# Leading tokens' and context's chains in another order, and three tiles' sums read later

## The reference

```python
y, k, v = token_mixer(h, ...)
x = x + gt1 * rmsnorm(y, g_post_mix)
h = rmsnorm(x, g_pre_ffn) * (1 + sc2) + sh2
aff = softmax(h @ w_router)                 # token x expert
g, idx = top_k(aff.T, cap)                  # cap 64 of 512 latents, 16 of 128 context tokens
hid = silu(xe @ w_gate) * (xe @ w_up)       # xe = h[idx]; width 2816
out = zeros.at[idx].add((hid @ w_down) * g)
x = x + gt2 * rmsnorm(out, g_post_ffn)
```

## Time and profile before

| | |
|---|---|
| time, median of 3 runs | 1947.46 us (1947.1 to 1952.33) |
| time of the profiled execution | 1953.02 us |
| its span, first to last instruction | 1951.2 us |
| PE busy | 1910.8 us, 98% of the span |
| DVE, ACT, POOL busy | 459.4, 301.4, 144.7 us |
| moved by DMA | 644.51 MB, mean 330 GB/s |

### The profile page before, as it was taken

How to read it: one execution, slowest core, us unless ns; L and a number is a source line. 1 busy time by engine, 2 the same in 40 slices (tenths; PEclk the granted TensorE clock), 3 DMA queues, 4 the chain that set the end, 5 groups by cost and what they waited for, 6 DMA issues and landing times.

```text
span 1951.2 us, 36708 instructions
## 1 busy us (share of the span) xinstructions
PE 1910.8 (98%) x16641; PEld 888.6 (46%) x16641; DVE 459.4 (24%) x825; ACT 301.4 (15%) x548; POOL 144.7 (7%) x216
## 2 busy tenths in 40 slices
PE   6999999999979999999999999999999999999997
PEld 3889787779853333323333333333333333333322
DVE  3432355557352101111010111101111110110114
ACT  4222245444220000000000000000000000000001
POOL 1000000000121101001010100101010010100004
PEclk9999999999979999999999999999999999999999
DMA  8851111112569999999999999999999999999997
GB/s 350 336 198 63 46 50 55 44 53 88 233 262 366 412 420 413 418 414 419 413 412 420 413 418 414 419 414 413 420 412 417 414 418 407 413 414 413 418 400 290
DMA packets 101412, 644.51 MB, mean 330 GB/s; under 512 B 11760, under 2 KB 14208, under 8 KB 43408
## 3 DMA queue, kind: packets, MB, share of 16 engines
q1 hardware_dynamic: 93792, 618.23, 77.5%
q0 software_dynamic: 6608, 20.85, 3.4%
q10 hardware_dynamic: 864, 3.15, 0.4%
HBM read 625.66 MB, written 16.52 MB: 329 GB/s over the span
## 4 chain that ended last, share of the span: by engine, by line
PE 96%; DVE 1%; DMA 1%; POOL 1%; issue 0%; ACT 0%; SPq 0%; POOLq 0%; DVEq 0%; ACTq 0%
PE ps L892 94%; PE ps L1073 1%; DMA out<-fin 1%; DMA x<-in_x_sample 0%; PE ps L995 0%; PE ps L1210 0%; PE ps L900 0%; PE ps L929 0%; DVE Gs L1921 0%; POOL rsx L733 0%; DVE topi L2095 0%; POOL rsx L732 0%; DVE topv L2094 0%; PE ps L1103 0%; DVE work L2097 0%
## 5 line engine op out<-in xcount | busy, mean ns | idle before, releaser
L892 PE MATMUL ps<-ring,xeT 128*32 128x512 f32 (+1 forms) x9216 | 914.4, 557 | 0.0
L892 PEld LDWEIGHTS ps<-ring,xeT 128*32 128x32 f32 x9216 | 296.9, 110 | 609.8 <-issue 608.5
L892 PE MATMUL ps<-ring,hidT 128*32 128x512 f32 x4224 | 459.6, 592 | 3.1 <-DMA ring<-in_w_dn 3.1
L892 PEld LDWEIGHTS ps<-ring,hidT 128*32 128x32 f32 x4224 | 136.1, 110 | 317.4 <-issue 310.8
L2233 DVE TENSOR_TENSOR hid<-sil,ps 128x768 f32<-128x768 f32 (+1 forms) x48 | 42.6, 887 | 915.1 <-ACT sil L1708 915.1
L1708 ACT ACTIVATE sil<-ps 128x768 f32<-128x768 f32 (+1 forms) x48 | 36.4, 758 | 959.9 <-PE ps L892 959.9
L892 PE MATMUL ps<-hT_hi,gq_hi 128*128 128x320 f32 x256 | 88.1, 344 | 0.0
L892 PE MATMUL ps<-in_hi,hT_hi 128*128 128x384 f32 x240 | 82.2, 343 | 0.0
L892 PE MATMUL ps<-in_lo,hT_hi 128*128 128x384 f32 x240 | 80.4, 335 | 0.0
L892 PE MATMUL ps<-in_hi,hT_lo 128*128 128x384 f32 x240 | 80.3, 335 | 0.0
L892 PE MATMUL ps<-hT_hi,gq_lo 128*128 128x320 f32 x256 | 79.1, 309 | 0.0
(11 more groups left out here) (262 smaller groups left out, 1432.0 us busy)
## 6 DMA issues: line engine op xcount, KB each, us to landing
ring<-in_w_gu SPq DMA_DIRECT2D x256, 1024.0 KB, 27.1
ring<-in_w_dn SPq DMA_DIRECT2D x176, 1024.0 KB, 24.1
ring<-in_w_gu_rest SPq DMA_DIRECT2D x128, 768.0 KB, 24.1
slab_y<-in_w_mod_blocks SPq DMA_DIRECT2D x8, 2048.0 KB, 8.9
in_slab<-in_w_in_blocks SPq DMA_DIRECT2D x6, 1536.0 KB, 8.7
gq<-in_w_gates SPq DMA_DIRECT2D x16, 512.0 KB, 3.4
slab<-in_w_mod_blocks SPq DMA_DIRECT2D x3, 2048.0 KB, 16.3
x<-in_x_sample SPq DMA_DIRECT2D x8, 512.0 KB, 6.4
```

The source lines that it names most:

```text
L892: return pe.matmul(out, lhsT, rhs, start=first, stop=last, **kw)
```

## The change

The diff has these parts.

- `aff_T(2)` and `aff_T(3)` are called after 4 of `out_proj(4)`'s 16 steps, not after 5.
- The first round of choice reads the affinities from PSUM and writes `work` by its replace; the copy goes. `row_list(0)` comes ahead of the fourth round's replace, and no longer waits for `y_done`, since its list `fG` lies elsewhere.
- Tile 4: ACT copies the projection unscaled (`y_copied`) ahead of squaring it, the square's dump goes to `xq[0]`; POOL issues `gather(0)` ahead of `rstd`; POOL only multiplies by the gain; DVE scales and adds the residual in one instruction, between rounds 5 and 6 (the rounds count from 0). ACT makes both halves of `h2T`.
- `first_tokens(0)` is done ahead of round 7, `first_tokens(2)` ahead of the tables' copies.
- `first_gate_up` has 16 units of group 0 first, then 8 + 4 of group 1, then group 2.
- At the end ACT loads the sums of tiles 2, 3 and 4 and the row of gains behind the first two tiles' squares, the last SILU, and the landing of load 556 of 0 to 559.

```diff
             for i, t in enumerate(LATE):
-                pool.wait_ge(y_sq, i + 1)
-                rstd(rsy[:, i:i + 1], ssy[:, i:i + 1], D, EPS).then_inc(y_rs, 1)
                 if t == NL:
...
                     gather(0, first_gathered)
+                pool.wait_ge(y_sq, i + 1)
+                rstd(rsy[:, i:i + 1], ssy[:, i:i + 1], D, EPS).then_inc(y_rs, 1)
+                if t == NL:
                     pool.wait_ge(gg_ev, 4)
-                    pool.wait_ge(y_scaled, 1)
+                    pool.wait_ge(y_copied, 1)
                     pool.tensor_tensor(row[0][:, :], row[0][:, :], ggrow[:, 1, :], ALU.mult).then_inc(y_used, 1)
-                    pool.wait_ge(ld_x[NL], 32)
-                    pool.wait_ge(y_used, NT)
-                    pool.tensor_tensor(x1[:, home(NL), :], x1[:, home(NL), :], row[0][:, :], ALU.add).then_inc(x1_ready, 1)
...
             def first_gate_up():
                 pe.wait_ge(x_add, 1)
-                first_part(0, range(1), (0,))
+                first_part(0, range(3), (0,))
                 second_rows()
-                first_part(0, range(1, 3), (0,))
                 router(NT - 1)
-                first_part(0, range(3, 7), (0,))
+                first_part(0, range(3, 6), (0,))
                 aff_T(NT - 1)
-                first_part(0, range(7, KD), (0,))
-                first_part(1, range(2), (0,))
+                first_part(0, range(6, KD), (0,))
+                first_part(1, range(5), (0,))
                 context_rows()
-                first_part(1, range(2, 4), (0,))
+                first_part(1, range(5, KD), (0,))
                 pe.wait_ge(x_add, 2)
                 first_part(0, range(4), (1,))
                 tables_T()
                 first_part(0, range(4, KD), (1,))
+                first_part(1, range(4), (1,))
                 pe.wait_ge(x_add, 3)
                 first_part(0, range(KD), (2,))
-                for k in range(KD):
-                    first_part(1, (k,), (1, 2) if k < 4 else (0, 1, 2))
+                first_part(1, range(4), (2,))
+                first_part(1, range(4, KD), (1, 2))
...
-            for t in LAST:
+            def sums_rows(t):
                 act.wait_ge(w_used, FREE + t // 2)
                 act.dma_start(fin[t][:, :], ysum_dram[t * P:(t + 1) * P, :]).then_inc(ld_x[t], 16)
+            for t in LAST[:2]:
+                sums_rows(t)
+            act.wait_ge(xs_ready, E_)
+            for i in range(2):
+                tokens_square(i)
+            silu(last, 2)
+            late = len(FLOW_W) - 4
+            act.wait_ge(w_ld[late % RS], 16 * (late // RS + 1))
+            for t in LAST[2:]:
+                sums_rows(t)
             act.wait_ge(gg_loaded, 16)
             act.wait_ge(w_used, FREE + 3)
             rows = gg_dram[KD:2 * KD, :].rearrange("(o k) p -> o (k p)", o=1)
             act.dma_start(gg_c[:, :], rows.to_broadcast([P, D])).then_inc(gg_loaded, 16)
-            act.wait_ge(xs_ready, E_)
-            for i in range(2):
-                tokens_square(i)
-            silu(last, 2)
             for i in range(2, NT):
                 tokens_square(i)
...
-            for r in range(4):
+            v8, i8, all_ = topv[:, 0:8], topi[:, 0:8], ps[0:E_, 7, :]
+            link(dve.max(v8, all_))
+            link(dve.max_index(i8, v8, all_))
+            link(dve.match_replace(work[:, :], v8, all_, -1.0))
+            dve.sem_inc(affT_used, 1)
+            for r in range(1, 4):
+                choose(work, LAT, 0, r, r < 3)
+            row_list(0)
+            v8 = topv[:, 24:32]
+            link(dve.match_replace(work[:, :], v8, work[:, :], -1.0))
+            first_index(0)
+            for r in range(4, 6):
                 choose(work, LAT, 0, r, True)
-            dve.wait_ge(y_done, NT)
-            row_list(0)
...
+            dve.wait_ge(ld_x[NL], 32)
+            dve.wait_ge(y_rs, NT)
+            dve.wait_ge(y_used, NT)
+            dve.scalar_tensor_tensor(x1[:, home(NL), :], row[0][:, :], rsy[:, 4:5], x1[:, home(NL), :],
+                                     ALU.mult, ALU.add).then_inc(x1_ready, 1)
+            choose(work, LAT, 0, 6, True)
             dve.wait_ge(first_gathered, 16)
             first_tokens(0)
+            choose(work, LAT, 0, 7, False)
             row_list(1)
-            h2_low(NT - 1)
```

More of the change, by code:

```diff
@@ L279, in program @@
         xs = at("xs", E0 + 47104, [P, 3, 256])
-        fG = at("fG", E0 + 11264, [E_, 3, 4, 32])
+        fG = [at("fG_lat", 117760, [E_, 2, 4, 32]), at("fG_ctx", E0 + 11264, [E_, 1, 4, 32])]
         yrA, yrB = at("yrA", E0 + 4096, [P, 512]), at("yrB", E0 + 6144, [P, 512])
@@ L302, in program @@
         topi = at("topi", 117440, [E_, CT], U32)
-        topf = at("topf", E0 + 49792, [E_, CT])
         S0 = [E0 + 53248]
@@ L326, in program @@
         work_c = small("work_c", [E_, CTX])
+        topf = small("topf", [E_, CT])
         idxT = small("idxT", [P, 3, E_], I32)
@@ L378, in program @@
             sem(n) for n in ("idxg_set", "idxs_set", "gathered", "scattered"))
-        first_gathered, first_turned, y_scaled = sem("first_gathered"), sem("first_turned"), sem("y_scaled")
+        first_gathered, first_turned, y_copied = sem("first_gathered"), sem("first_turned"), sem("y_copied")
         pool_turn = sem("pool_turn")
@@ L1255, in _ @@
             router(3)
-            out_proj(4, 3, 5)
+            out_proj(4, 3, 4)
             aff_T(2)
             aff_T(3)
-            out_proj(4, 5, 16)
+            out_proj(4, 4, 16)
             def rows_T(bank_, g):
-                return pe.transpose(ps[:, bank_, g * E_:(g + 1) * E_], fG[:, g, :, :].rearrange("e x j -> e (x j)"),
+                return pe.transpose(ps[:, bank_, g * E_:(g + 1) * E_], fG[g // 2][:, g % 2, :, :].rearrange("e x j -> e (x j)"),
                                     par[0:E_, 0:E_])
@@ L1647, in y_square @@
                 b = 2 * (i % 2)
-                act.activation(row[i % 2][:, :], ps[:, b:b + 2, :].rearrange("p b n -> p (b n)"), ACT.Square, scale=0.5,
+                if i == NT - 1:
+                    act.wait_ge(x2_stored[0], 32)
+                dump = xq[0] if i == NT - 1 else row[i % 2]
+                act.activation(dump[:, :], ps[:, b:b + 2, :].rearrange("p b n -> p (b n)"), ACT.Square, scale=0.5,
                                accum_out=ssy[:, i:i + 1]).then_inc(y_sq, 1)
@@ L1691, in _ @@
             l_exp(3)
+            act.wait_ge(y_done, NT)
+            act.activation(row[0][:, :], ps[:, 0:2, :].rearrange("p b n -> p (b n)"), ACT.Copy).then_inc(y_copied, 1)
             y_square(4)
-            act.wait_ge(y_rs, NT)
-            act.activation(row[0][:, :], ps[:, 0:2, :].rearrange("p b n -> p (b n)"), ACT.Copy,
-                           scale=rsy[:, 4:5]).then_inc(y_scaled, 1)
             x1_square(4)
             h2_high(4)
+            act.activation(h2T[0][:, 0:4, :], ps[:, 4, :].rearrange("p (k t) -> p k t", k=4), ACT.Copy).then_inc(h2_v, 1)
             quarters(4)
@@ L2117, in _ @@
             dve.wait_ge(affT_done, NL)
-            dve.tensor_copy(work[:, :], ps[0:E_, 7, :]).then_inc(affT_used, 1)
-            dve.wait_ge(affT_used, 1)
             def scaled(c, g0, g1):
@@ L2142, in row_list @@
                 for x in range(4):
-                    last = dve.tensor_scalar(fG[:, g, x, :], topi[:, 32 * g:32 * g + 32], 4.0, float(x), ALU.mult, ALU.add)
+                    last = dve.tensor_scalar(fG[0][:, g, x, :], topi[:, 32 * g:32 * g + 32], 4.0, float(x), ALU.mult, ALU.add)
                 link(last)
@@ L2149, in first_index @@
                 dve.tensor_copy(idx_g[g][:, :], ps[:, 7, g * E_:g * E_ + 1]).then_inc(idxg_set, 1)
-            for r in range(4):
-                choose(work, LAT, 0, r, True)
-            dve.wait_ge(y_done, NT)
-            row_list(0)
[L2155 to L2161, removed]
+            v8, i8, all_ = topv[:, 0:8], topi[:, 0:8], ps[0:E_, 7, :]
[10 more added lines that the diff above has]
+            for r in range(4, 6):
+                choose(work, LAT, 0, r, True)
+            dve.wait_ge(ld_x[NL], 32)
[4 more added lines that the diff above has]
+            choose(work, LAT, 0, 6, True)
             dve.wait_ge(first_gathered, 16)
             first_tokens(0)
+            choose(work, LAT, 0, 7, False)
             row_list(1)
-            h2_low(NT - 1)
             first_index(1)
@@ L2177, in _ @@
                 for n in range(2):
-                    last = dve.tensor_scalar(fG[:, 2, x, CC * n:CC * (n + 1)], topi[:, CL:CT], 4.0, float(4 * LAT + x),
+                    last = dve.tensor_scalar(fG[1][:, 0, x, CC * n:CC * (n + 1)], topi[:, CL:CT], 4.0, float(4 * LAT + x),
                                              ALU.mult, ALU.add)
@@ L2197, in _ @@
             dve.sem_inc(tab_ready, 1)
+            dve.wait_ge(gathered, 16)
+            first_tokens(2)
             dve.wait_ge(tabT_done, 4)
@@ L2207, in _ @@
             dve.wait_ge(tab_set, 1)
```

(2 more changed lines are left out.)

## The result

The changed kernel took 1964.59 us (median of 4 executions, 1961.66 to 1966.31), the kernel before, beside it, 1949.55 us (4, 1947.10 to 1952.33). The ratio is 1.0071, with an interval from 1.0051 to 1.0091. So the change costs about 14 us. The forecast said slower, by 9.2 us, and put the end of its range at 1962.0 us; the measured median is 2.6 us above that. A later comparison with more executions gave 1.0074 (1.0059 to 1.0090). The profiled execution took 1966.31 us with a span of 1964.5, against 1953.02 and 1951.2 before: 13.3 us more span.

What follows compares the result with a forecast made beforehand. The saturated weight stream was taken as the bound, PE living on a shrinking cushion. Late rows cost 9.2 us, containing the front's gain of 0.7 and the stream's lateness of 4.1: median 1947.5 to 1956.7 us, range 1946.5 to 1962.

Steps and rivals of the forecast that it cites:

- Cost of this part: 1946.5 + 13.9: At the end, late rows: tile 4 finished at 1946.5, then 13.9 us of work to 1960.4, 9.2 us more.
- SP issues a load when the slot 18 loads back is used up, so at PE's pace: Weight stream: loads issued at PE's pace but delivered ever later, 6.0 us at load 18, 25.3 at load 545.
- Some comes back: Front: of load 18's delay, 0.9 us return by a faster landing, 1.3 us by gathers and load 17's tail.
- The first slots given back: First expert: eight more units delay load 18 from 597.5 to 603.8; the stream runs 4.1 us late.
- The forecast's term for the clock: PE's first units after the new idle time: slower at 1.2 GHz, costing 0.3 us, bounds 0 to 1.6.
- Covers: Rest of the front: later second list, gather 1, context's list and h2T's half on ACT, all costed at nothing.
- `finish` of tile 4 takes 2.5 us on DVE after that.: Near the end: once the late rows' transfers end at 1944.0, DVE finishes tile 4 in 2.5 us, at 1946.5.
- 13.9 us of work in a row: After tile 4's finish to the span's end: 18.5 us before, less idle times of 3.9 and 0.7 us.
- Load 559 about 1939, PE's end about 1945: Last weights: last load lands about 1939, PE ends about 1945 and is no longer on the path.
- What would show it: Signs, among them load 18 near 604, load 545 landing over 27 us after issue, last rows 12 us behind load 556.
- No measurable change: Rival, chance 0.30: DMA engines have room at the end, so late rows pass; time within 0.3%, 1948 to 1952.5.
- Faster, because PE is the bound: Rival, chance 0.06: weights in time, front's gain and 3.1 us of end waits come through; 3.8 to 5.1 us less.

Runs made afterwards that it cites:

- front_only: The changed kernel with the sums' rows and gains loaded ahead of the squares, as before the change; ratio 1.0033 to the kernel before.
- chains_only: The changed kernel with the order of units in first_gate_up and the loads of the sums' rows as before; ratio 1.0006 to the kernel before.
- tail_only: The kernel before with only the sums' rows and gains loaded late; ratio 1.0048 to the kernel before.
- rows_at_silu: The changed kernel without the wait for load 556, the late rows going right after the last SILU; ratio 1.0041 to the kernel before.
- units_only: The kernel before with only the new order of units in first_gate_up; ratio 1.0047 to the kernel before.
- extra_store: The kernel before with four more stores of 0.52 MB to unused memory, ahead of load 140; ratio 1.0040 to the kernel before.
- after_again: The changed kernel once more, for more executions; ratio 1.0074 to the kernel before.

## Why the prediction was right and wrong

The direction and the two causes, a late stream and late rows, came out. What failed is the sum at the end, and the place that it started from. The forecast was 9.2 us of span, the profile shows 13.3, and the difference is made of these sizes:

| step | forecast | measured | off |
|---|---|---|---|
| load 556 landed, rows go | 1928.8 | 1930.3 | +1.5 |
| load 556 to the gains' landing | 15.2 us | 15.4 us | +0.2 |
| gains' landing to `finish` of tile 4 | 0 | 1.2 us | +1.2 |
| `finish` of tile 4 | 2.5 us | 2.5 us | 0 |
| from there to the span's end | 13.9 us | 15.0 us | +1.1 |

Their sum is 4.0, and 9.2 + 4.0 is the measured 13.3 but for rounding. From 1956.7 to 1964.59 it is 7.9 us: 4.1 are these sizes, 3.0 the starting point (the median of three executions was 1947.5, that of twenty 1950.5), and 0.8 are left, since the medians lie further apart than the two profiles. The sizes alone would have given 1960.8, the starting point alone 1959.7; only together do they pass 1962, and the forecast's own slow bound of 1962.9 lay beyond that already.

**The step that failed** is "Cost of this part: 1946.5 + 13.9". It put two chains at nothing: the one behind tile 4's row (measured 1.2 us) and the one through POOL's scatters (1.1 us). Load 556, 1.5 us later than in the sum, is the third term. Of this 1.5, the stream's lateness is 1.0, and about 0.5 come from the rows that moved: without them loads 545 to 556 were to land closer together by 5.0 us, and did by 4.4 (27.9 us in place of 32.3).

**One hit is partly luck.** From load 556 to the gains' landing the sum took 12.5 us of transfer at 416 GB/s, 5.2 MB. The trace has fewer bytes at a lower rate, 4.3 MB at 282 GB/s:

```profile
1930.34:1945.75 15.41, 10.47 (x79) 2.60 (x76) 4.50 (x4) 3.99 (x7) 2.06 (x5) 0.78 0.72 282
```

The two errors cancel to 0.2 us.

**"SP issues a load when the slot 18 loads back is used up, so at PE's pace"** holds for load 18, but not for load 545, which the argument compares with it. PE had used up load 527, whose slot load 545 takes, by 1862.3, and load 545 went out only at 1872.08, 9.8 us later. And the time from issue to landing does not grow along the kernel: it is 6.0 us for load 18, 16.8 for load 28 and 23.4 for load 49, but then 17.2 for load 64, 32.9 for load 360 and 25.3 for load 545. The conclusion, that the stream loses ground to PE, is right all the same; what shows it is the cushion. In the kernel before, load 18 landed 22.3 us before PE had used up the load ahead of it (by the count of `w_used`), load 210 16.4 us, load 360 10.9 and load 545 8.7.

**The mis-sized term of the front is "Some comes back" under "The first slots given back".** Load 18's issue was right (603.8 forecast, 603.50 measured), and so was its flight (5.1 and 4.8 us). What was wrong is what falls into the gap: 1.3 us for gathers and load 17's tail. The stream's lateness at load 545 is 5.1 us, not 4.1. With load 18 issued 6.0 us later and landing in 1.2 us less, 4.8 of lateness remain, and the traffic that was to fall into the gap gave nothing back. The 4.8 and the measured 5.1 agree without it. The bounds of 3.0 and 5.5 held it.

**The front's chains.** The residual's end (570.0 forecast, 569.66), gather 0's issue (564.2, 563.95), its landing (570.5, 570.4) and the new wait before the first unit (1.7, 1.58) came out. MAX8 from PSUM took 0.69 us. PE's gain was 0.7 us in the forecast. The first unit began 1.35 us earlier, and three units took 4.31 us in place of 3.60, so 0.6 are left; with the wait of 0.2 us that is gone, it is the 0.9 us by which PE is early at load 545. They did not help: the kernel is slower. The forecast's term for the clock, 0.3 us with bounds of 0 and 1.6, measured 0.7 in the changed kernel, 1.7 in front_only (5.34 less 3.60) and 2.0 in chains_only: the clock can take the whole gain, which the bound left out.

**Covers.** The wait of three units in front of the second list was costed at nothing. Gather 1 was issued at 578.21, before at 576.93, and load 16 at 588.52, before at 588.05: 0.5 us, inside the lateness above.

**"`finish` of tile 4 takes 2.5 us on DVE after that."** This started `finish` at the landing of the gains. The row of tile 4 has a chain of its own behind its landing: square on ACT (1944.03 to 1945.2), two steps on POOL (to 1946.95), then DVE. With one row landed 12.8 us after issue, at 1944.0, this chain ends behind the gains' landing (1945.7). That chain was not followed in the forecast. 0.85 us of it are POOL's first step, which took 1.04 us in place of 0.19, beside DVE's finish of the tile ahead (the last section has the rows).

**"13.9 us of work in a row".** That number took DVE's rows before, less their idle time for PE. But with no idle time the context's two scatters on POOL (1.34 and 0.84 us) stand ahead of the latents' 1/rms. POOL takes it up at 1958.88, though DVE's part of it was ready at 1957.55, and DVE waits 1.95 us where it waited 0.74. Idle time that is taken out of a chain can have been another engine's cover. tail_only and the changed kernel both have 15.0 us.

**The weights' end.** "Load 559 about 1939, PE's end about 1945": PE's last piece began at 1940.23, and it ended at 1948.9 because the clock was at 0.50 from 1940 to 1945. It cost the changed kernel nothing, since DVE came to it only at 1951.20. In front_only and rows_at_silu, where PE is the end of the chain, it did cost: 7.84 and 9.03 us for 6.21.

**What would show it.** Load 18 near 604, no idle time of DVE behind tile 4, and the last rows 12 us or more behind load 556 (13.7 and 15.4) were seen. One sign was mistaken: load 545 was to land over 27 us after its issue, but took 25.4, as before. Its issue moved by 5.0 us along with everything else, since SP itself is held up. Load 545's slot was free at 1861.4, before at 1862.3, and it went out 15.7 us after that, before 9.8; SP's row for it lasts 2.1 us in the kernel before, where that of load 18 lasts 0.33. Lateness in a saturated stream shows in absolute times, not in the time from issue to landing. PE's wait before tile 4's transposes was to be 2.7 us shorter. The transposes came 3.0 us sooner, yet the wait is only 1.0 shorter, since it now begins earlier: the other wait of 2.3 us stood ahead of it and is gone.

**The rivals.** "No measurable change" rested on the DMA engines having room at the end (share 0.76). The window of the changed kernel from 1930 to 1935 us has share 0.87 with the late rows in it, but each further row took 3.2 and 2.5 us (landing at 1938.3, 1941.5 and 1944.0) where 0.52 MB take 1.26 at the stream's rate. They did not pass beside the other queue; they shared. From 1940.3 to 1943 us the rows' queue (q10) and SP's (q1) moved about as many packets:

```profile
q10 hardware_dynamic: 85, 0.30, 27.5%
q1 hardware_dynamic: 66, 0.24, 21.5%
```

The Trainium skill's rule in "DMA: Bandwidth & Descriptors", section "Queues, rings and completion order", that an engine goes round between queues packet by packet, fits that, and fits PE's waits in rows_at_silu. It is not the whole of it: in those 2.7 us the engines were only about half busy and moved 206 GB/s in all. Why a row still took 2.5 us stays open. "Faster, because PE is the bound" is refuted by units_only, where no unit of PE is added and only slots come back later, and by extra_store, where PE gets nothing to do at all. In tail_only PE waits 2.0 us less for weights, and the time grows.

One thing stands in the profile of before that the forecast did not use. The last chain there does not come from PE's last matmul but, by 0.1 us, from POOL: its scatters of the context wait for the store of tile 4, issued at 1932.76 and landed 10.4 us later, and they end at 1945.56, where DVE's part of the latents' 1/rms is ready at 1945.46.

```profile
1943.47 0.94 POOL L881 DMA_INDIRECT out<-yrB,idx_oB  x1 [1.63 <-DMA out<-fin]
```

So by this profile two things set the end of that kernel together, PE's last matmul and that store. In the changed kernel the store took 2.6 us, and nothing waited for it.

## What to carry to other kernels

An engine at 100% and full clock is not the bound if the cushion of its prefetched loads, from landing to use, shrinks along the kernel (here from 22.3 to 8.7 us): then the stream is, and every microsecond in which it idles, and every byte that it carries anywhere, comes out at the end. The time from issue to landing is a poor sign of it: here it was as long at load 49 as at load 545. In such a kernel judge a change of the first loop by when it gives back the first slot, not by when it begins. And a transfer moved behind a late load takes its whole consumer chain with it, landing, square, 1/rms and finish, including what two engines did at the same time as long as there was idle time between them.

## What the runs showed of the hardware

- Behind waits for weights at the very end, PE's granted clock fell in some profiles and not in others. In the changed kernel waits of 1.74 and 3.20 us, with 8 matmuls between them, were followed by 0.50 in the window below, and the last 56 matmuls took 8.63 us; after_again had waits of 1.85 and 3.32 us and 7.67 us. In the kernel before, with 1.09 and 1.40 us, the clock stayed at 1.00: 6.21 us. But 0.86 and 1.40 us gave 7.84 us in front_only and 6.22 in units_only, so the length of these two waits alone does not decide it. What does stays open.

```profile
1935.00:1940.00 5.00, 1.06 (x8) 0.16 (x8) 0.00 (x0) 1.15 (x2) 0.32 (x2) 0.83 0.70 274
1940.00:1945.00 5.00, 4.77 (x24) 1.19 (x28) 3.79 (x3) 2.12 (x4) 1.25 (x3) 0.50 0.62 253
```

- The rounds' operations cost the same from PSUM as from SBUF within 0.01 us. Over 16 x 512, MAX8 took 0.69 and 0.68 us, FIND_INDEX8 0.68 and 0.67, MATCH_REPLACE8 0.67 and 0.66 to 0.67.
- POOL's steps of 1/rms on 128 x 1, mostly 0.19 and 0.55 us, took longer when they began while DVE ran one of the two instructions of `finish` (128 x 1024, both inputs in SBUF), and ended only after it. The one of 1.04 us in the changed kernel began at 1945.27 and ended 0.05 us behind DVE's, which ran from 1945.04 to 1946.27. The kernel before has four such steps, of 0.96, 1.54, 1.28 and 1.54 us:

```profile
1927.24 1.28 POOL L732 TENSOR_SCALAR rsx<-ssx 128x1 f32<-128x1 f32 x1
1928.61 1.54 POOL L733 TENSOR_TENSOR rsx<-rsx,mhalf 128x1 f32<-128x1 f32 x1
```

- The phase ahead of the experts, the same in these kernels but for its last instructions, differed by 6.5 us from one profile to another (555.8 to 562.3), with a granted clock from 300 to 560 us of 1.00 in units_only and chains_only (555.8 to 555.9), 0.99 in front_only (558.6), and 0.97 before and after (562.3).
